# Expert stage: the choice of later experts ahead of the gate multiply on VectorE

## The chip, the cores and the metric

The kernel runs on one core of a Trainium2 chip. The metric is the time of one execution on the device, in microseconds (us). The kernel before takes 2801.93 us, the median of three runs (2798.73 to 2804.31). One execution was also profiled; rows of that profile are quoted below.

## What is computed

Two layers over 512 tokens (256 context, 256 latent). Each layer has an attention mixer and then a "PEER" expert stage. Only the second is touched here. For each token and each of 8 heads it finds the best 16 of 16,384 experts by two small searches, and sums over them:

```python
v1, i1 = lax.top_k(s1, PEER_TOPK)
v2, i2 = lax.top_k(s2, PEER_TOPK)
cand = (v1[..., :, None] + v2[..., None, :]).reshape(...)
cand_idx = (i1[..., :, None] * PEER_N_KEYS + i2[..., None, :]).reshape(...)
top_s, top_pos = lax.top_k(cand, PEER_TOPK)
expert_idx = jnp.take_along_axis(cand_idx, top_pos, axis=-1)
gates = jax.nn.softmax(top_s, axis=-1)
a = jax.nn.gelu(jnp.einsum('td,thkd->thk', tc, u_tab[ec]), approximate=False)
return jnp.einsum('thk,thkd->td', gc * a, v_tab[ec])
```

`tc` are the token's 1024 values, `ec` the chosen experts, `gc` their gates. Layer 0 does this for all 512 tokens, layer 1 for the 256 latent ones.

## The kernel before, in words

Tokens lie in chunks of 128, one token per partition. A **unit** is one head of one chunk: 16 experts per token. Layer 0 has 8 heads x 4 chunks = 32 units, layer 1 has 8 x 2 = 16, so 48 in all. Each layer's units run in a hardware loop of 4 passes (`Fori`, 8 units a pass in layer 0, 4 in layer 1). A unit's 16 experts go in 4 **groups** of 4.

The order of work is written out by hand, engine by engine, with semaphores between them:

- **POOL** (GpSimd, L833) gathers for each expert slot 128 rows of 2048 floats: 1024 of table u and 1024 of table v. The ring holds 16 slots, exactly one unit. A group's four slots are asked for again once TensorE has finished with the group (`slots_free`, L830).
- **DVE** (VectorE) does in each group four dot products of u rows with the token (L1118, each leaves a result by a short accumulator read), then waits for ScalarE's Gelu and multiplies the four values with the gates (L1124, which counts `w_ready` up), and then does one of four parts of `choose` for the unit after the next (L1125): part 0 searches the two score rows (L1019 to L1023, L1031), part 1 the 16 x 16 sums (L1033 to L1037), part 2 turns positions into indices (L1041 to L1044), part 3 forms the expert index and releases POOL (L1046 to L1049). After the fourth group it finishes the gates (L1053, L1054), copies scores where there are new ones (L1058), waits until TensorE has done the fourth group (L1131), and adds the unit's result to x (L1134, L1137).
- **ACT** (ScalarE) does the Gelu (L979) when the dots are there, waits for `w_ready`, and scales the identity by the four weights (L984): four diagonal matrices, kept for two groups.
- **PE** (TensorE) multiplies the diagonals with the v rows, 8 matmuls of 512 columns a group (L924), summing in two banks over the unit. Each such fp32 matmul stands in the profile as two instructions. Behind group 0 it also does one query projection (L886) and behind group 2 the scores (L894) in those units that have such a job (`job_of`, L763: chunk number under 2). That is 16 of the 32 units of layer 0, and all 16 of layer 1, where the projection is half as wide.

Of the kernel before, what the change touches and what calls it, by code (L numbers as in the profile page):

```python
# [42 lines left out]
def kind(c):  # L43
    return CON if c < CC else LAT
# [12 lines left out]
class Kernel:  # L57
# [637 lines left out]
    def peer(self, layer, chunks):  # L695
# [65 lines left out]
        place = [divmod(i, nch) for i in range(body + 2)]  # L761

        def job_of(i, it):  # L763

            hd, c = place[i]
            return it * 4 + (2 * hd + c + first_jobs) if c < 2 else None
# [14 lines left out]
        with nc.Block() as block:  # L781
# [221 lines left out]
            def _(dve):  # L1003
                count = [0]

                def link(ins):

                    count[0] += 1
                    ins.then_inc(chain, 1)
                    dve.wait_ge(chain, count[0])  # L1010

                def restart():

                    dve.sem_clear(chain)
                    count[0] = 0

                def top16(out_v, out_i, src):

                    link(nc.vector.max(out_v[:, 0:8], src))  # L1019
                    link(nc.vector.max_index(out_i[:, 0:8], out_v[:, 0:8], src))  # L1020
                    link(nc.vector.match_replace(src, out_v[:, 0:8], src, NEG))
                    link(nc.vector.max(out_v[:, 8:16], src))  # L1022
                    link(nc.vector.max_index(out_i[:, 8:16], out_v[:, 8:16], src))  # L1023

                def choose(par, c, u, stage):

                    if stage == 0:
                        for side in range(2):
                            top16(val[:, side, :], ind[:, side, :], scores[:, par, c, side * NKEY:(side + 1) * NKEY])  # L1030
                        link(nc.vector.tensor_copy(indf, ind))  # L1031
                    if stage == 1:
                        link(nc.vector.tensor_tensor(C, val[:, 0, :].unsqueeze(2).broadcast_to([P, TOPK, TOPK]),  # L1033
                                                     val[:, 1, :].unsqueeze(1).broadcast_to([P, TOPK, TOPK]), ALU.add))
                        top16(top, pos, C.rearrange("p a b -> p (a b)"))
                        link(nc.vector.tensor_scalar(posi[:, 0, :], pos, 4, None, ALU.logical_shift_right))
                        link(nc.vector.tensor_scalar(posi[:, 1, :], pos, TOPK - 1, None, ALU.bitwise_and))  # L1037
                    if stage == 2:
                        for side in range(2):

                            link(nc.vector.tensor_tensor(OH, posi[:, side, :].unsqueeze(2).broadcast_to([P, TOPK, TOPK]),  # L1041
                                                         iota.unsqueeze(1).broadcast_to([P, TOPK, TOPK]), ALU.is_equal))
                            link(nc.vector.tensor_tensor(OH, OH, indf[:, side, :].unsqueeze(1).broadcast_to([P, TOPK, TOPK]), ALU.mult))
                            link(nc.vector.tensor_reduce(sel[:, side, :], OH, AX.X, ALU.add))  # L1044
                    if stage == 3:
                        link(nc.vector.scalar_tensor_tensor(out=idx[:, u, :], in0=sel[:, 0, :], scalar=float(NKEY), in1=sel[:, 1, :], op0=ALU.mult, op1=ALU.add))  # L1046
                        dve.sem_inc(idx_ready, 1)
                        link(nc.vector.tensor_scalar(nb, top[:, 0:1], -1.0, None, ALU.mult))
                        dve.sem_inc(top_ready, 1)  # L1049

                def finish_gates(u):

                    link(nc.vector.reciprocal(er, es))  # L1053
                    link(nc.vector.tensor_scalar(gate[:, u, :], gate[:, u, :], er, None, ALU.mult))  # L1054

                def copy_scores(j, par, side):
                    dve.wait_ge(sc_done, j + 1)
                    nc.vector.tensor_copy(scores[:, par, 0:nch, side * NKEY:(side + 1) * NKEY],  # L1058
                                          S_BANK[:, 0:nch * NKEY].rearrange("p (c n) -> p c n", c=nch)).then_inc(sc_copied, 1)
                    dve.wait_ge(sc_copied, j + 1)  # L1060
# [48 lines left out]
                with dve.Fori(0, H // 2) as it:  # L1109
                    for i in range(body):  # L1110
                        u = i % 2
                        hd, c = place[i]
                        unit = it * body + i
                        j = job_of(i, it)
                        for g in range(NG):
                            for k in range(g * GRP, (g + 1) * GRP):
                                dve.wait_ge(gathered[k], unit * 16 + 16)
                                last = nc.vector.tensor_tensor_reduce(  # L1118
                                    out=ring[:, k, 0:D], in0=ring[:, k, 0:D], in1=self.h[:, chunks[c] * D:(chunks[c] + 1) * D], scale=1.0, scalar=0.0,
                                    op0=ALU.mult, op1=ALU.add, accum_out=a[:, u, k:k + 1])  # L1120
                            last.then_inc(dots_done, 1)
                            ks = slice(g * GRP, (g + 1) * GRP)
                            dve.wait_ge(gelu_done, unit * NG + g + 1)
                            nc.vector.tensor_tensor(w[:, u, ks], w[:, u, ks], gate[:, u, ks], ALU.mult).then_inc(w_ready, 1)  # L1124
                            choose(place[i + 2][0] % 2, place[i + 2][1], u, g)  # L1125
                        dve.wait_ge(exp_done, unit + 3)
                        finish_gates(u)
                        if j is not None:
                            copy_scores(j, (hd + lead) % 2, c)

                        dve.wait_ge(slots_free, unit * NG + 2 * NG)  # L1131
                        for n in range(2):
                            s = acc[u][n][:]
                            link(nc.vector.tensor_tensor(s, s, gate_f[:, kind(chunks[c]), n * 512:(n + 1) * 512], ALU.mult))  # L1134
                        for n in range(2):
                            xs = self.x[:, chunks[c], n * 512:(n + 1) * 512]
                            link(nc.vector.tensor_tensor(xs, xs, acc[u][n][:], ALU.add))  # L1137
                        dve.sem_inc(acc_free, 1)
                        restart()
# [270 lines left out]
```

## Time and profile before

| | |
|---|---|
| median of the runs | 2801.93 us |
| the profiled execution | 2804.31 us, its span 2804.3 us |
| expert loop of layer 0, 32 units | 1454.5 us |
| expert loop of layer 1, 16 units | 719.8 us |
| PE busy over the span | 2139.2 us (76%) |
| DVE busy over the span | 1769.5 us (63%) |
| busy share of the DMA engines in the loops | 0.92 and 0.90 |

A row of the costliest groups reads: line, engine, operation, out<-in, shape, xcount | busy us, mean ns of one | idle us of the engine just before them, and what ended most of it.
### The profile page before, as it was taken

The numbers are of one execution on the slowest core, as the hardware profiler recorded it, in microseconds if no ns is written. First come the engines' busy times: TensorE is split into PE (matmuls) and PEld (weight loads), VectorE is DVE, ScalarE is ACT, GpSimd is POOL, SyncE is SP. The second block draws the span as 40 slices with busy tenths as digits, with TensorE's granted clock in tenths as the row PEclk, the third lists the DMA queues.
The fourth block names the chain that finished last, engine by engine and source line by source line (L and its number), as shares of the span: only waits on it lengthen the run. The fifth ranks groups of instructions, "written<-read, shape, count | busy, mean of one in ns | idle before, by whom it ended". The sixth has DMA issues, their size and how long they took to land. (4 is left out here: it accounts for less than half of the span.)

```text
span 2804.3 us, 21155 instructions
## 1 busy us (share of the span) xinstructions
PE 2139.2 (76%) x5856; PEld 1008.5 (36%) x5856; DVE 1769.5 (63%) x4349; ACT 581.5 (21%) x1533; POOL 887.9 (32%) x774
## 2 busy tenths in 40 slices
PE   5899978678686878686867768678857868687776
PEld 2444443233233333232323323334533424243333
DVE  1233466867676767667585777645466767768685
ACT  1222122121112212121211121222212212122122
POOL 0000024443434434344343343400034434343431
PEclk8999989898888989898988888888968989898888
DMA  7467369998989999899998998942179999999995
GB/s 314 146 236 267 126 244 366 392 380 355 416 332 385 377 380 391 355 358 395 361 386 359 363 412 355 377 176 94 39 301 401 387 373 382 387 381 391 372 390 216
DMA packets 136073, 919.71 MB, mean 328 GB/s; under 512 B 15744, under 2 KB 20864, under 8 KB 30128
## 3 DMA queue, kind: packets, MB, share of 16 engines
q0 software_dynamic: 110592, 805.36, 71.0%
q1 hardware_dynamic: 24960, 113.03, 10.7%
q8 instruction: 24, 0.39, 0.1%
q14 instruction: 65, 0.53, 0.0%
q10 hardware_dynamic: 432, 0.40, 0.0%
HBM read 917.58 MB, written 1.15 MB: 328 GB/s over the span
## 5 line engine op out<-in xcount | busy, mean ns | idle before, releaser
L924 PE MATMUL bank<-arena,aux 128*128 128x512 f32 x3072 | 1462.6, 634 | 543.3 <-ACT aux L984 543.0
L833 POOL DMA_INDIRECT arena<-in_uv,small x768 | 887.4, 1155 | 1386.3 <-PE bank L924 1079.4
L924 PEld LDWEIGHTS bank<-arena,aux 128*128 128x128 f32 x3072 | 616.2, 204 | 1353.5 <-issue 735.8
L1118 DVE CUSTOM_DVE_ANT_0 arena<-arena,h 128x1024 f32<-128x1024 f32 x768 | 897.8, 1223 | 57.0 <-issue 36.0
L979 ACT ACTIVATE small<-small 128x4 f32<-128x4 f32 x192 | 39.5, 206 | 1466.2 <-DVE small L1118 1466.2
L984 ACT ACTIVATE aux<-ident,small 128x128 f32<-128x128 f32 x768 | 245.2, 390 | 59.6 <-DVE small L1124 58.1
L1134 DVE TENSOR_TENSOR bank<-bank,aux 128x512 f32<-128x512 f32 x96 | 67.2, 700 | 278.0 <-PE bank L924 276.3
L886 PE MATMUL bank<-hT,aux 128*128 128x512 f32 (+1 forms) x512 | 170.3, 486 | 0.0
L822 POOL IOTA small<- 128x16 int32 x2 | 0.3, 135 | 479.2 <-POOLq L53 479.2
L886 PEld LDWEIGHTS bank<-hT,aux 128*128 128x128 f32 x512 | 97.3, 190 | 74.7 <-issue 68.9
L1053 DVE RECIPROCAL small<-small 128x1 f32<-128x1 f32 x52 | 8.5, 164 | 133.7 <-ACT small L992 120.7
L847 PE MATMUL bank<-arena,hT 128*128 128x512 f32 x192 | 85.1, 603 | 3.3 <-PEq L53 3.3
L1124 DVE TENSOR_TENSOR small<-small 128x4 f32<-128x4 f32 x192 | 31.3, 163 | 73.3 <-ACT small L979 73.3
L457 PE MATMUL bank<-arena 128*128 128x512 f32 (+1 forms) x160 | 68.3, 544 | 2.1 <-PEq L53 1.4
L1137 DVE TENSOR_TENSOR x<-x,bank 128x512 f32<-128x512 f32 x96 | 65.9, 686 | 3.3
L979 ACT ACT_TABLE_LOAD x48 | 61.6, 1283 | 1.8 <-PE bank L879 1.0
L1118 DVE DVE_READ_ACCUMULATOR2_ANT small<- 128x1 f32 x768 | 61.9, 81 | 0.0
L992 ACT ACT_TABLE_LOAD x48 | 61.6, 1283 | 0.8
L532 DVE TENSOR_REDUCE small<-bank 128x1 f32<-128x512 f32 (+1 forms) x48 | 28.9, 601 | 50.7 <-PE bank L457 50.7
L1224 PE MATMUL bank<-arena,hT 128*128 128x512 f32 x128 | 58.0, 612 | 2.9 <-ACT hT L243 2.9
L656 PE MATMUL bank<-arena 128*128 128x512 f32 x128 | 56.3, 593 | 0.8 <-DVE arena L608 0.8
L1022 DVE MAX8 small<-aux 128x8 f32<-128x128 f32 x156 | 52.9, 339 | 5.4
(143 smaller groups left out, 1430.0 us busy)
## 6 DMA issues: line engine op xcount, KB each, us to landing
h<-in_ada SPq DMA_DIRECT2D x27, 1024.0 KB, 6.0
arena<-in_ada SPq DMA_DIRECT2D x21, 1024.0 KB, 6.5
aux<-in_w_query SPq DMA_DIRECT2D x36, 512.0 KB, 13.3
arena<-in_uv,small POOLq DMA_INDIRECT x768, 14.4
arena<-mod_rows SPq DMA_DIRECT2D x17, 512.0 KB, 7.0
arena<-in_w_o SPq DMA_DIRECT2D x2, 4096.0 KB, 12.3
arena<-in_w_qkv SPq DMA_DIRECT2D x3, 2048.0 KB, 10.3
arena<-in_w_in SPq DMA_DIRECT2D x2, 1536.0 KB, 8.7
```

Of the source, the lines that this page charges most:

```text
L457: last = nc.tensor.matmul(self.bank[S_BANK[u % 2]][:, 0:keys_of(c)], q, k, start=(i == 0), stop=(i == len(terms) - 1))
L833: nc.gpsimd.indirect_dma_start(out=ring[:, k, :], out_offset=None, in_=table, in_offset=bass.IndirectOffsetOnAxis(ap=idx[:, i % 2, k:k + 1 ...
L847: last = nc.tensor.matmul(self.bank[2 * (i % 2) + n][:], self.hT[:, hd, c * P:(c + 1) * P], self.w_o[:, hd, n * 512:(n + 1) * 512], start= ...
L886: last = nc.tensor.matmul(Q_BANK[:, lo:hi], wq[:, k, :], self.hT[:, k, lo:hi], start=(k == 0), stop=(k == KD - 1))
L924: last = nc.tensor.matmul(acc[i % 2][n][:], diag[:, (g % 2) * GRP + k, :], ring[:, kk, D + n * 512:D + (n + 1) * 512], start=(kk == 0), st ...
L979: nc.scalar.activation(w[:, u, ks], a[:, u, ks], ACT.Gelu).then_inc(gelu_done, 1)
L984: last = nc.scalar.mul(diag[:, (g % 2) * GRP + k, :], self.ident[:], w[:, u, g * GRP + k:g * GRP + k + 1])
L992: nc.scalar.activation(gate[:, u, :], top, ACT.Exp, bias=nb, accum_out=es).then_inc(exp_done, 1)
L1118: last = nc.vector.tensor_tensor_reduce(out=ring[:, k, 0:D], in0=ring[:, k, 0:D], in1=self.h[:, chunks[c] * D:(chunks[c] + 1) * D], scale= ...
L1134: link(nc.vector.tensor_tensor(s, s, gate_f[:, kind(chunks[c]), n * 512:(n + 1) * 512], ALU.mult))
L1137: link(nc.vector.tensor_tensor(xs, xs, acc[u][n][:], ALU.add))
L1224: last = nc.tensor.matmul(self.bank[3 * (i % 2) + n][:], self.hT[:, k, c * P:(c + 1) * P], self.w_qkv[:, n, k, :], start=(k == 0), stop=(k ...
```

## The change

In every group of a unit DVE does its part of `choose` first, and waits for the Gelu and multiplies afterwards. The two statements change places; nothing is added or taken away.

```diff
--- before.py
+++ after.py
@@ -1120,9 +1120,9 @@
                                     op0=ALU.mult, op1=ALU.add, accum_out=a[:, u, k:k + 1])
                             last.then_inc(dots_done, 1)
                             ks = slice(g * GRP, (g + 1) * GRP)
+                            choose(place[i + 2][0] % 2, place[i + 2][1], u, g)
                             dve.wait_ge(gelu_done, unit * NG + g + 1)
                             nc.vector.tensor_tensor(w[:, u, ks], w[:, u, ks], gate[:, u, ks], ALU.mult).then_inc(w_ready, 1)
-                            choose(place[i + 2][0] % 2, place[i + 2][1], u, g)
                         dve.wait_ge(exp_done, unit + 3)
                         finish_gates(u)
                         if j is not None:
```

Only DVE's order differs. In group 0 of a unit, before (the first row reads the last accumulator, ISA and REGISTER_ALU rows at L1123 or L1124 are the wait's register work, L1019 is the first row of part 0 of the choice):

```order
 L1118 ISA small 128x1
-L1123 ISA
-L1124 TENSOR_TENSOR small<-small 128x4
-L1019 MAX small<-aux 128x8
-L1020 MAX_INDEX small<-small,aux 128x8
```

and in the changed kernel, the end of the same part of the choice:

```order
+L1022 MAX small<-aux 128x8
+L1023 MAX_INDEX small<-small,aux 128x8
+L1031 CAST small<-small 128x32
+L1124 ISA
+L1125 TENSOR_TENSOR small<-small 128x4
```

The multiply (now L1125) moved behind all eleven instructions of part 0. In group 3, in the waits' own view of DVE (the names in brackets are semaphores; `chain_105` orders DVE behind itself), the multiply moved behind the two instructions of part 3:

```order
-L1123 REGISTER_ALU
-L1124 TENSOR_TENSOR small<-small 128x4 [waits gelu_done_101]
 L1046 SCALAR_TENSOR_TENSOR small<-small 128x16
 L1048 TENSOR_SCALAR small<-small 128x1 [waits chain_105]
-L1126 REGISTER_ALU [waits chain_105]
+L1124 REGISTER_ALU [waits chain_105]
+L1125 TENSOR_TENSOR small<-small 128x4 [waits gelu_done_101]
+L1126 REGISTER_ALU
 L1053 RECIPROCAL small<-small 128x1 [waits exp_done_107]
```

Behind the multiply follow, as before, the wait for the exponentials and the gates (L1053, L1054). The instructions of the other engines and their order stay as they were.

## Rows read from the trace of the kernel before

**Rows 1.** The page's part of the costliest groups; columns in the section on the profile.

```profile
L924 PE MATMUL bank<-arena,aux 128*128 128x512 f32 x3072 | 1462.6, 634 | 543.3 <-ACT aux L984 543.0
...
L1118 DVE CUSTOM_DVE_ANT_0 arena<-arena,h 128x1024 f32<-128x1024 f32 x768 | 897.8, 1223 | 57.0 <-issue 36.0
...
L1134 DVE TENSOR_TENSOR bank<-bank,aux 128x512 f32<-128x512 f32 x96 | 67.2, 700 | 278.0 <-PE bank L924 276.3
...
L1124 DVE TENSOR_TENSOR small<-small 128x4 f32<-128x4 f32 x192 | 31.3, 163 | 73.3 <-ACT small L979 73.3
```

**Rows 2.** Windows of both expert loops; busy (xcount) by engine, clock, DMA share, GB/s.

```profile
400.90:1855.40 1454.50, 1093.02 (x2432) 473.21 (x2432) 1030.00 (x2512) 291.57 (x784) 575.67 (x496) 0.88 0.92 370
2074.60:2794.40 719.80, 545.68 (x1344) 264.18 (x1344) 514.50 (x1264) 148.26 (x403) 278.81 (x240) 0.88 0.90 366
```

**Rows 3.** Timeline of PE, layer 0; start, us, engine line op [idle before].

```profile
999.37 9.75 PE L924 MATMUL bank<-arena,aux 128*128 128x512 f32 x16 [9.88 <-ACT aux L984]
1008.95 7.03 PE L886 MATMUL bank<-hT,aux 128*128 128x512 f32 x16
1015.82 13.90 PE L924 MATMUL bank<-arena,aux 128*128 128x512 f32 x32
...
1030.44 7.03 PE L924 MATMUL bank<-arena,aux 128*128 128x512 f32 x16
1047.36 16.51 PE L924 MATMUL bank<-arena,aux 128*128 128x512 f32 x32 [9.88 <-ACT aux L984]
1064.67 7.13 PE L924 MATMUL bank<-arena,aux 128*128 128x512 f32 x16 [0.80 <-ACT aux L984]
...
1089.43 16.05 PE L924 MATMUL bank<-arena,aux 128*128 128x512 f32 x32 [9.87 <-ACT aux L984]
```

**Rows 4.** Timeline of DVE over one unit, layer 0.

```profile
1040.75 1.28 DVE L1118 CUSTOM_DVE_ANT_0 arena<-arena,h 128x1024 f32<-128x1024 f32 x1 [0.36 <-DVE x L1137]
...
1045.75 0.16 DVE L1124 TENSOR_TENSOR small<-small 128x4 f32<-128x4 f32 x1 [0.27 <-ACT small L979]
1045.83 0.29 DVE L1019 MAX8 small<-aux 128x8 f32<-128x128 f32 x1
...
1049.72 1.23 DVE L1118 CUSTOM_DVE_ANT_0 arena<-arena,h 128x1024 f32<-128x1024 f32 x1
...
1054.74 0.42 DVE L1033 TENSOR_TENSOR aux<-small 128x256 f32<-128x256 f32 x1
...
1058.13 1.23 DVE L1118 CUSTOM_DVE_ANT_0 arena<-arena,h 128x1024 f32<-128x1024 f32 x1
...
1063.15 0.42 DVE L1041 TENSOR_TENSOR aux<-small 128x256 f32<-128x256 uint32 x1
...
1065.88 1.22 DVE L1118 CUSTOM_DVE_ANT_0 arena<-arena,h 128x1024 f32<-128x1024 f32 x1
...
1070.83 0.16 DVE L1124 TENSOR_TENSOR small<-small 128x4 f32<-128x4 f32 x1 [0.27 <-ACT small L979]
...
1071.23 0.15 DVE L1048 TENSOR_SCALAR small<-small 128x1 f32<-128x1 f32 x1 [0.15 <-DVE small L1046]
...
1079.60 1.43 DVE L1134 TENSOR_TENSOR bank<-bank,aux 128x512 f32<-128x512 f32 x2 [4.80 <-PE bank L924]
```

**Rows 5.** Timeline of DVE, group 2 of the unit before it.

```profile
1016.74 0.16 DVE L1124 TENSOR_TENSOR small<-small 128x4 f32<-128x4 f32 x1 [1.90 <-ACT small L979]
```

**Rows 6.** Windows, the first matmuls after an idle PE.

```profile
1047.36:1052.50 5.14, 5.14 (x6) 2.18 (x7) 4.90 (x15) 0.00 (x0) 0.00 (x0) 0.50 1.02 425
```

**Rows 7.** Timeline of PE, layer 1, first group of two units.

```profile
2125.36 9.95 PE L924 MATMUL bank<-arena,aux 128*128 128x512 f32 x16 [9.88 <-ACT aux L984]
...
2263.84 8.98 PE L924 MATMUL bank<-arena,aux 128*128 128x512 f32 x16 [15.31 <-ACT aux L984]
```

**Rows 8.** Timeline of POOL, last gather issued for that unit.

```profile
1042.02 1.97 POOL L833 DMA_INDIRECT arena<-in_uv,small  x1 [0.30 <-issue]
```

**Rows 9.** The page's DMA issues; count, median us to landing.

```profile
arena<-in_uv,small POOLq DMA_INDIRECT x768, 14.4
```

## The prediction

> **What bounds the kernel now.** I read the costliest groups first, then windows over the two expert loops, then the timelines of TensorE (PE) and VectorE (DVE) over neighbouring units.
>
> In the costliest groups the reader is to see who waits for whom [rows 1]. PE stands idle 543.3 us ahead of its expert matmuls, nearly all until ScalarE's diagonals (L984) are there. DVE stands idle 276.3 us ahead of L1134, until PE has done a unit's last group. Its 768 dot products have only 57.0 us of idle ahead of them, 36.0 of it at the restarts of the loop. So PE and DVE wait for each other in turn, and DVE hardly ever waits for a gather, though the DMA engines are busy 0.92 and 0.90 of the two loops [rows 2].
>
> The PE timeline gives the shape of a unit [rows 3]. After 9.88 us of idle PE starts group 0 at 999.37. Then come the projection at 1008.95, groups 1 and 2 from 1015.82, and group 3 from 1030.44 to its end at 1037.5, with the short scores between: one train without a gap, 38 us long. So in a unit with a projection nothing but the start of group 0 and PE's own work sets the end. In the next unit, without a projection, groups 0 and 1 are back to back (1047.36, 16.51 us), and groups 2 and 3 come after gaps such as 0.80 us, when DVE's multiply has made them ready.
>
> In the layer 0 loop 16 of 32 units have a projection. In layer 1 all 16 do, at half the width. I call these 32 units P and the other 16 units N.
>
> **What moves.** The multiply of group 0 starts at 1045.75, 0.27 us of idle after the dots, and PE starts 1.61 us behind it, at 1047.36 [rows 3, 4]. Part 0 of the choice runs from 1045.83 to the next dot at 1049.72, so it takes 3.89 us; part 1 is 1054.74 to 1058.13, 3.39; part 2 is 1063.15 to 1065.88, 2.73; part 3 is about 0.5 (1070.9 to 1071.38) [rows 4]. In the changed kernel the Gelu is long done when a part of the choice is over. The multiply of group 0 then comes 3.89 later and saves the 0.27 of waiting: a shift of **+3.62 us**, and the start of PE's group 0 shifts by as much.
>
> For the later groups, count through DVE's chain from a unit's first dot (1040.75). Before, the multiplies are at 5.0, 13.9, 22.3 and 30.1. After, each group saves its wait of 0.27 us and each multiply stands behind its own part of the choice: about 8.6, 16.8, 24.4 and 29.6. The first three are later by 3.6, 2.9 and 2.1; the last is earlier by 0.5.
>
> **Units P, 32 of them.** Their train has no gap before. After, it starts 3.62 later, and the diagonals are ready 1.6 us behind each multiply, at 18.4, 26.0 and 31.2. PE wants group 1 only behind group 0 and the projection. Group 0 takes at least 6.87 us (half of the gapless 13.90 of groups 1 and 2, less the modelled tail), and the projection 3.5 in layer 1. Even so group 1 can't start before 10.2 + 10.4 = 20.6, so the train stays whole. In layer 0 the Gelu of group 2 stands on ScalarE behind the copy of the projection, as before, where it made DVE wait 1.90 us [rows 5]. I put the multiply of group 2 there at about 27 and of group 3 at 33, which with 1.6 is still far ahead of group 3's turn at about 41. DVE's other work at the unit's end (exponentials, gates, scores) is done while it now waits for PE, and stays so. So 32 x 3.62 = **+115.8 us**.
>
> **Units N, 16 of them.** Before: DVE starts L1134 at 1079.60, 38.85 after the first dot, with PE paced by DVE's multiplies for groups 2 and 3. After: PE starts group 0 at 10.2. The two groups of 16.51 us (16.35 without the tail) and two more at 13.90 end at 10.2 + 16.35 + 13.90 = 40.5. With the shorter first pair at 1089.43 (16.05, of which a fraction was waiting for the diagonals) it is at most 40.0, and with the least slow start seen (below) 39.7. The diagonals of groups 1 to 3 (18.4, 26.0, 31.2) come at PE's turn or ahead of it, so the train becomes gapless and PE takes over as the bound. I take 40.2, so +1.4 each: 16 x 1.4 = **+22 us**. The ends are 39.7 (+0.9, 14 us) and, with the slowest start seen, 40.6 (+1.8, 28 us).
>
> **The slow start of PE.** The first 5.14 us after an idle PE run at a granted clock of 0.50, the 1.2 GHz level [rows 6]; before them the engine had been idle 9.88 us. That lengthens group 0 from 7.03 to 9.75 or 9.95 us, or to 8.98 in the shortest such row [rows 3, 7]: 1.95 to 2.92 us a unit, paid already in each of the 48. After the change the idle ahead of group 0 is 9.88 + 3.62 = 13.5 us. The row of 8.98 has 15.31 us of idle ahead of it, at a restart of the loop, and is no longer than the others. So I change nothing for it in the sum. The bounds are all starts at the least (1.95, against the middle of the two, 2.45: 48 x -0.5 = -24 us) and all at the most (48 x +0.5 = +24 us).
>
> The Trainium skill, "TensorE: Matmul & The Clock Gate", section "HAM oscillation — how this bites in real kernels", has it that each idle gap makes the next burst start cold, so that the cost goes with the number of gaps. By that rule the sum stands as it is; by a cost that grows with the gap it would be the rival on the cold start below. The two rows of layer 1 speak for the rule.
>
> **What hides it, or doesn't.** Gathers: the last gather of this unit is issued at 1042.02 and its dot starts about 1069.3, 27 us later, against a median of 14.4 to land [rows 4, 8, 9]. PE frees the groups later by 3.6 and the next unit begins later by 3.6 too, so the distance stays in P units. In N units it shrinks by up to 3 us for group 1 (freed 3.8 later, its next dots 0.9 later). The spare of about 10 us covers it. Besides, longer units ask less of the DMA engines. I put nothing in the sum; if it were not covered, the loss would be those 3 us in 16 units, +48.
>
> **Sum.** 115.8 + 22 = +138 us. Against the profiled execution (2804.31, its span 2804.3) this is 2942; its own time lies 2.4 above the median of the runs, so against the median of 2801.93 it is **2940 us**. Changes within 0.2% (5.6 us) would be no change that a measurement of this kernel can tell.
>
> **Rivals.**
>
> *The DMA engines set the pace.* At 0.92 busy they look like the most contended resource, and the order on DVE would cost nothing as long as the ring is refilled: 2802 us. For it speaks the share in rows 2. Against it speaks the idle ahead of the dots [rows 1], 57.0 us over 768 with 36.0 at restarts. The Trainium skill, "Perfetto Trace Analysis", section "Identifying the Most-Contended Engine", says to improve the resource with the highest use, for DMA by HBM utilization; no row here shows what these DMA engines can reach at most. By it alone this rival would be the forecast.
>
> *The last multiply decides (the other side).* The multiply of group 3 comes 0.5 us earlier, because four waits for the Gelu of 0.27 leave DVE's chain and part 3 of 0.5 goes in front. If each unit ended 8.8 us behind that multiply, as N units do now, every unit would be 0.5 shorter: 48 x -0.5 = -24, 2778 us. It decides from the point at which PE has a gap ahead of group 3 in spite of the later start. For it: the gap of 0.80 in the N unit [rows 3]. Against: P units have none, and in N units the start's delay of 3.6 is larger than the gaps, 0.80 and a similar one.
>
> *The cold start grows with the gap.* If the slow stretch grows as the idle does, 13.5 / 9.88, the 2.45 us become 3.35: 48 x 0.9 = +43, 2983 us. Against it is the row of 8.98.
>
> *Gathers run late in N units:* +48, 2988 us, argued above.
>
> **Chances.** My forecast 0.85; the cold start 0.06; gathers late 0.04; DMA paces 0.02; the last multiply decides 0.02, the rest 0.01 for something unseen that slows. The range holds the forecast with its bounds (24 either way for the slow start, -8 and +6 for N units) and stops short of both +43 and +48: 2912 to 2972. Slower by over 0.2% 0.96, within 0.2% 0.02, faster 0.02.
>
> **What would show it.** In the changed kernel's profile each step has its row. The idle of PE ahead of group 0 goes from 9.88 to 13.5. PE's groups 2 and 3 in N units lose their gaps. The wait of DVE ahead of the multiply falls from 73.3 us in all to that of the 16 P units of layer 0 only, some 2.5 each, 40 us. The wait of DVE ahead of L1134 rises by 3.6 to 4 in P units and by about 2 in N, from 276.3 to some 430. The loops grow to about 1535 and 778 us. The forecast is wrong if PE shows gaps behind group 0 in P units, if the matmuls at 0.50 last longer than 5.8 us a unit, or if idle until a gather stands ahead of L1118.

## The result, and the profile after

The changed kernel takes 2938.80 us (median of 4 runs, 2936.03 to 2940.17) against 2801.45 us before (4 runs). The ratio is 1.049, with a 95% interval of 1.0476 to 1.0505: 137 us slower. The forecast was 2940 us.

Costliest groups of the changed kernel, the same columns as in [rows 1]; the multiply is now L1125. L1053 and L1058 are VectorE's other two waits at a unit's end, for the exponentials and for the scores:

```profile
L924 PE MATMUL bank<-arena,aux 128*128 128x512 f32 x3072 | 1453.7, 634 | 689.5 <-ACT aux L984 689.5
...
L1118 DVE CUSTOM_DVE_ANT_0 arena<-arena,h 128x1024 f32<-128x1024 f32 x768 | 897.0, 1223 | 53.2 <-issue 37.3
...
L1134 DVE TENSOR_TENSOR bank<-bank,aux 128x512 f32<-128x512 f32 x96 | 67.2, 699 | 315.4 <-PE bank L924 313.8
...
L1053 DVE RECIPROCAL small<-small 128x1 f32<-128x1 f32 x52 | 8.5, 164 | 163.7 <-ACT small L992 161.6
L1058 DVE COPY aux<-bank 128x512 f32<-128x512 f32 (+1 forms) x32 | 17.9, 558 | 127.7 <-PE bank L894 127.7
...
L1125 DVE TENSOR_TENSOR small<-small 128x4 f32<-128x4 f32 x192 | 31.4, 164 | 77.8 <-ACT small L979 50.8
```

TensorE's idle until the diagonals grew by 146 us (543.3 to 689.5). The dots still wait for nothing: 53.2 us of idle, 37.3 of it at the loops' restarts.

Windows of the two expert loops, as in [rows 2]:

```profile
397.70:1935.00 1537.30, 1088.13 (x2432) 479.26 (x2432) 1017.76 (x2512) 291.45 (x784) 520.54 (x496) 0.85 0.87 350
2154.50:2928.70 774.20, 541.60 (x1344) 263.03 (x1344) 509.86 (x1264) 146.73 (x403) 252.11 (x240) 0.85 0.84 341
```

Layer 0 grew by 82.8 us, layer 1 by 54.4, together 137.2: all of the loss is here. Engines do the same work in more time, and the DMA engines are less busy (0.87 and 0.84).

Timeline of TensorE over the same three units as in [rows 3], one with a projection and two without:

```profile
1034.46 9.66 PE L924 MATMUL bank<-arena,aux 128*128 128x512 f32 x16 [13.51 <-ACT aux L984]
1043.96 7.03 PE L886 MATMUL bank<-hT,aux 128*128 128x512 f32 x16
1050.83 13.90 PE L924 MATMUL bank<-arena,aux 128*128 128x512 f32 x32
1064.56 1.05 PE L894 MATMUL bank<-aux 128*128 128x128 f32 x8
1065.45 7.03 PE L924 MATMUL bank<-arena,aux 128*128 128x512 f32 x16
1086.00 30.10 PE L924 MATMUL bank<-arena,aux 128*128 128x512 f32 x64 [13.51 <-ACT aux L984]
1129.61 30.48 PE L924 MATMUL bank<-arena,aux 128*128 128x512 f32 x64 [13.52 <-ACT aux L984]
```

The idle ahead of group 0 went from 9.88 to 13.51 us. In a unit without a projection the 64 matmul instructions of the four groups are now one train, 30.1 to 30.5 us; the gaps ahead of groups 2 and 3 are gone.

### The profile page after: what moved, and what is told of

Read it like the earlier page. It is cut to its first block and busy times, and to the rows that moved or that the text cites. A ratio compares the mean times of both kernels' runs of the same rounds, so it can differ in the third digit from the quotient of the medians.

```text
span 2938.4 us, 21011 instructions
## 1 busy us (share of the span) xinstructions
PE 2127.4 (72%) x5856; PEld 1013.0 (34%) x5856; DVE 1753.0 (60%) x4349; ACT 579.9 (20%) x1533; POOL 806.0 (27%) x774
## 5 line engine op out<-in xcount | busy, mean ns | idle before, releaser
L924 PE MATMUL bank<-arena,aux 128*128 128x512 f32 x3072 | 1453.7, 634 | 689.5 <-ACT aux L984 689.5
L833 POOL DMA_INDIRECT arena<-in_uv,small x768 | 805.5, 1049 | 1597.8 <-PE bank L924 1295.6
L1118 DVE CUSTOM_DVE_ANT_0 arena<-arena,h 128x1024 f32<-128x1024 f32 x768 | 897.0, 1223 | 53.2 <-issue 37.3
L1134 DVE TENSOR_TENSOR bank<-bank,aux 128x512 f32<-128x512 f32 x96 | 67.2, 699 | 315.4 <-PE bank L924 313.8
L1053 DVE RECIPROCAL small<-small 128x1 f32<-128x1 f32 x52 | 8.5, 164 | 163.7 <-ACT small L992 161.6
L1058 DVE COPY aux<-bank 128x512 f32<-128x512 f32 (+1 forms) x32 | 17.9, 558 | 127.7 <-PE bank L894 127.7
L1125 DVE TENSOR_TENSOR small<-small 128x4 f32<-128x4 f32 x192 | 31.4, 164 | 77.8 <-ACT small L979 50.8
```

The lines of the kernel that those rows point to most:

```text
L833: nc.gpsimd.indirect_dma_start(out=ring[:, k, :], out_offset=None, in_=table, in_offset=bass.IndirectOffsetOnAxis(ap=idx[:, i % 2, k:k + 1 ...
L924: last = nc.tensor.matmul(acc[i % 2][n][:], diag[:, (g % 2) * GRP + k, :], ring[:, kk, D + n * 512:D + (n + 1) * 512], start=(kk == 0), st ...
L1118: last = nc.vector.tensor_tensor_reduce(out=ring[:, k, 0:D], in0=ring[:, k, 0:D], in1=self.h[:, chunks[c] * D:(chunks[c] + 1) * D], scale= ...
```

## The experiments

The theory: VectorE's time costs only where TensorE's train waits for it. That is at group 0 in every unit, and at groups 1 to 3 only where TensorE has a gap. Rivals: each swapped group, or each unit, pays its own share; the gathers pace the kernel. Each time is the median of four or five executions; ratios and differences are to the kernel before on the same chip. The diffs are shorthand: `C(g)` is the choice's part of group g, `M(g)` the wait for the Gelu with the multiply, and names are shortened. In the variants some line numbers shift. "Read from the trace" means the time from one unit's first matmul to the next unit's, against the same unit of the kernel before, averaged over a kind of unit.

**Group 0 alone.**

```diff
-M(g); C(g)
+if g == 0: C(g); M(g)
+else:      M(g); C(g)
```

> Only in group 0 of each unit the choice goes ahead of the multiply; groups 1 to 3 are as before. Theory (the start of TensorE's train is what costs): a unit's train starts 3.62 us later and is gapless behind that, so this one swap costs as much as all four: about +137 us, 2938 us, ratio to before 1.049. Rival (each swapped group adds its share by holding the diagonals back): group 0 has 3.9 of the 10.5 us of choice in a unit, so about 0.37 of the loss, +51 us, 2852 us, ratio 1.018.

Measured: 2941.55 us, ratio 1.0495 (1.0477 to 1.0514), +138 us. One group of four costs as much as all four. Its timeline has the same train with the same idle ahead of it:

```profile
1090.80 30.10 PE L924 MATMUL bank<-arena,aux 128*128 128x512 f32 x64 [13.51 <-ACT aux L984]
```

The rival with shares is out.

**Groups 1 to 3 alone.**

```diff
-M(g); C(g)
+if g > 0: C(g); M(g)
+else:     M(g); C(g)
```

> The choice goes ahead of the multiply in groups 1 to 3 only; group 0 is as before. Theory: units with a projection lose nothing, since TensorE's turn for groups 1 to 3 comes later than their diagonals even so (18.7, 26.2 and 31.6 us after the first dot against turns at 19.7, 26.6 and 33.9 in layer 1). In the 16 units without one group 1 starts at 18.7 in place of 15.5 and the train ends at 39.9 in place of 38.85: 16 x 1.05 = +17 us, 2818 us, ratio 1.006. Rival (every group its share): 0.63 of the loss, +86 us, 2888 us, ratio 1.031.

Measured: 2841.96 us, ratio 1.0134 (1.0114 to 1.0153), +39 us, and 1.0132 when it was run again. It is nearer to the theory than to the rival, but twice the +17 us. Read from the trace, the units with a projection lost about 0.1 us each and those without one 2.1 us, not 1.05. TensorE in one of the latter, by timeline and by windows (granted clock is the third figure from the end):

```profile
1059.25 9.57 PE L924 MATMUL bank<-arena,aux 128*128 128x512 f32 x16 [9.87 <-ACT aux L984]
1071.29 22.41 PE L924 MATMUL bank<-arena,aux 128*128 128x512 f32 x48 [2.47 <-ACT aux L984]
```

```profile
1071.30:1073.00 1.70, 1.70 (x2) 0.82 (x3) 1.70 (x3) 0.00 (x0) 1.40 (x2) 0.50 0.80 236
...
1075.00:1078.50 3.50, 3.50 (x9) 1.52 (x8) 3.24 (x9) 1.05 (x4) 0.58 (x1) 1.00 0.97 379
```

The later diagonals opened a gap of 2.47 us between groups 0 and 1, and group 1 began at the 1.2 GHz level, a second slow start in one unit. I had not reckoned with it. The trace has it in 14 of the 16 units, after gaps of 2.36 to 2.52 us. In the other two the gap was longer, 2.81 and 2.96 us, and group 1 took 7.13 us, at a granted clock of 1.00:

```profile
512.18 7.13 PE L924 MATMUL bank<-arena,aux 128*128 128x512 f32 x16 [2.81 <-ACT aux L984]
```

The two partial swaps do not add up to the whole (138 and 39 us against 137). Once group 0 starts late, the later groups' diagonals are there in time.

**The gap filled.** To test that, TensorE does three useless matmuls in that gap, in the kernel with groups 1 to 3 swapped.

```diff
+if j is None and g == 0:
+    for k in range(3):
+        matmul(Q_BANK[:, lo:hi], hT[:, k, 0:P], hT[:, k, lo:hi], start=(k == 0), stop=(k == 2))
```

> As the kernel with groups 1 to 3 swapped (2842 us), and in the 16 units without a projection TensorE does three more matmuls of 512 columns (six instructions, some 2.6 us, result used by nobody) in the gap of 2.47 us between groups 0 and 1. Theory (the gap let the granted clock fall to 0.50 again, which made group 1 take 8.4 us in place of 6.9, on top of its later start): without the gap group 1 runs at full clock, each of these units ends about 1.0 us earlier, 2842 - 16 = 2826 us, ratio to before about 1.008. Rival (group 1 is slow for another reason, such as gathers landing beside it or the diagonals): 2842 us or a little more, ratio 1.0135.

> The kernel with groups 1 to 3 swapped once more, on the same chip as the filled gap, to compare the two: 2842 us, ratio 1.0135.

Measured: 2823.87 us, ratio 1.0082 (1.0069 to 1.0096), against 2838.12 us and 1.0132 (1.0116 to 1.0147) without them. More work on TensorE made the kernel 14 us faster. Its timeline (L931 are the added matmuls):

```profile
1057.89 2.74 PE L931 MATMUL bank<-hT 128*128 128x512 f32 x6
1060.80 7.13 PE L924 MATMUL bank<-arena,aux 128*128 128x512 f32 x16 [0.17 <-ACT aux L987]
```

Group 1 takes 7.13 us now, at a granted clock of 1.00. Read from the trace, the units without a projection lost 2.0 us each without the added matmuls (2.1 in the first run) and 1.3 with them. So the second slow start was most of the missing 1 us a unit; what the remaining 0.2 us are stays open.

**Only the units without a projection**, all four groups swapped.

```diff
-M(g); C(g)
+if j is None: C(g); M(g)     # j is None: no projection in this unit
+else:         M(g); C(g)
```

> All four groups swapped, but only in the 16 units of layer 0 that have no projection. Theory: TensorE has gaps of 0.6 to 0.8 us ahead of groups 2 and 3 there, which take up most of the 3.62 us; what is left is about 1.5 us a unit, 16 x 1.5 = +24 us, 2825 us, ratio 1.0086. Rival (each unit loses its full shift): 16 x 3.62 = +58 us, 2859 us, ratio 1.021.

Measured: 2829.70 us, ratio 1.0095 (1.0078 to 1.0112), +26 us. This is the prediction's term of 22 us by itself, 4 us above it; the rival's 58 is out.

**Extra work behind the multiply.**

```diff
 M(g)
+if g == 0:
+    for _ in range(8): link(tensor_tensor(OH, C, C, ALU.max))
 C(g)
```

> The order of before, with eight more VectorE operations of 256 columns (0.46 us each, 3.66 together, their result is used by nobody) behind the multiply of group 0. Theory (VectorE's time costs only where TensorE's train waits for it): units with a projection in layer 0 lose nothing; in layer 1 the diagonals of group 3 come at 35.4 against a turn at 33.9, +1.4 each, 16 x 1.4 = 22; the 16 units without projection lose all of it, 16 x 3.66 = 59. Together +81 us, 2882 us, ratio 1.029. Rival (VectorE's time adds up in every unit, wherever it stands): 48 x 3.66 = +176 us, 2977 us, ratio 1.063.

Measured: 2895.67 us, ratio 1.033 (1.0314 to 1.0346), +92 us. By kind of unit, read from the trace as before: layer 0 with a projection +0.1 us each, layer 1 +1.9, without a projection +3.8. The same 3.66 us of VectorE cost nearly nothing in 16 units and all of themselves in 16 others. The 11 us beyond the forecast are 8 in layer 1, where I had set the diagonals against the slowest turn seen (33.9), not the mean one, and, in all, some 2 us in each of the two other kinds.

**Extra work ahead of the multiply**, in the changed kernel.

```diff
 C(g)
+if g == 0:
+    for _ in range(8): link(tensor_tensor(OH, C, C, ALU.max))
 M(g)
```

> The changed kernel with the same eight extra VectorE operations (3.66 us, result unused) ahead of the multiply of group 0, behind part 0 of the choice. Theory: now all 48 trains are gapless, so each unit ends later by the full 3.66: 48 x 3.66 = +176 us on the changed kernel, 3115 us, ratio to before 1.112. The slow start of TensorE stays at 1.9 to 2.9 us a unit although the idle ahead of it grows to 17 us. Rival (the slow start grows with the idle, in proportion): another 48 x 0.9 = +43 us, 3158 us, ratio 1.127. Rival (units without projection still have room): 32 x 3.66 = +117 us, 3056 us.

Measured: 3116.87 us, ratio 1.1116 (1.1099 to 1.1133), +313 us. With the change's own 137 us taken off, that leaves 313 - 137 = 176 us, on average 3.66 for each of the 48 units. Read from the trace it is 3.4 in layer 0 and 3.9 in layer 1: the idle ahead of group 0 grew by 3.67 (13.51 to 17.18), and the slow starts differ a little. TensorE over one unit without a projection:

```profile
1140.77 29.84 PE L924 MATMUL bank<-arena,aux 128*128 128x512 f32 x64 [17.18 <-ACT aux L984]
```

After 17.18 us of idle the train takes no longer than after 13.51. Over all units with a projection, group 0 took on average 9.49 us before, 9.45 in the changed kernel and 9.18 here in layer 0, and 9.60, 9.35 and 9.56 in layer 1. A cold start that grows with the gap is out.

**Taking the sum out later.** VectorE takes a unit's sum out of the banks behind group 0 of the next unit, once with the order of before and once with the changed one. The first call finds banks set to zero.

```diff
-dve.sem_inc(acc_free, 2)
+memset(acc[1][n], 0.0) for both n; dve.sem_inc(acc_free, 1)
 ...
+if g == 0:
+    take_out((i - 1) % body, unit * NG + NG)
 ...
-dve.wait_ge(slots_free, unit * NG + 2 * NG)
-(L1132 to L1138: the gate, the sum, acc_free)
+take_out(body - 1, H * nch * NG + NG)   # behind the loop
```

> The order of before, but VectorE takes a unit's sum out of the banks (L1134, L1137) behind group 0 of the next unit, not ahead of it. Theory (the hand-off at the unit's end, TensorE's 9.9 us of idle, is what a later start adds to): with it gone, VectorE's own chain is some 38 us a unit (34.1 to the gates, 3.3 for the sum, 1 for the scores) and the gathers some 42 (16.8 MB, and 17.3 with a projection, at the 391 GB/s of the busiest units), so the gathers take over as the bound: about 48 x 42.3 + 35 at the loops' restarts = 2065 us for the two loops in place of 2174, 2690 us in all, ratio 0.96. If gathers reach 425 GB/s it is VectorE, near 39.5 us a unit, and 2565 us. Rival (the gathers bound the kernel already, at a DMA share of 0.92): within 1% of before.

> The same later take-out, in the changed kernel's order. Theory: the 3.62 us on the start of a train are hidden, since TensorE is no longer what a unit ends with; within 1% of the kernel that takes out later with the order of before (about 2690 us), ratio to before about 0.96. Rival (the start of each train is paid for whatever comes ahead of it): 32 x 3.62 + 22 = +138 us above that kernel, 2828 us, ratio 1.01.

Measured: 2629.77 us, ratio 0.9377 (0.9364 to 0.939), with the order of before, and 2633.46 us, ratio 0.9392 (0.9379 to 0.9405), with the changed one. Both are 6% faster than the kernel before. The order that cost 137 us costs 4 here. The two intervals overlap, though all five times of the one (2627.83 to 2631.88) lie below all five of the other (2632.51 to 2636.44), so the 4 us may be real. The windows from 600 to 1600 us of the kernel before, and of this one with the order of before:

```profile
600.00:1600.00 1000.00, 747.98 (x1674) 324.76 (x1673) 698.13 (x1705) 200.06 (x535) 404.91 (x350) 0.88 0.93 373
```

```profile
600.00:1600.00 1000.00, 840.44 (x1827) 361.56 (x1826) 777.65 (x1889) 220.55 (x588) 410.15 (x384) 0.92 1.01 415
```

The costliest groups of the latter (L1133 are the dots):

```profile
L1133 DVE CUSTOM_DVE_ANT_0 arena<-arena,h 128x1024 f32<-128x1024 f32 x768 | 907.3, 1223 | 178.3 <-DMA arena<-in_uv,small 118.8
```

Now the dots wait for gathers, 118.8 us. The Trainium skill, "DMA: Bandwidth & Descriptors", section "Where 436 GB/s comes from", has it that transfers between HBM and SBUF are bound near 358 GB/s a core, which it works out as half of what the memory gives to two cores. This kernel runs on one core, and the 415 GB/s of this window are above that figure; the measurement decides.

## Why the prediction was right

**The start of group 0.** +3.62 us were worked out; the idle ahead of it grew by 3.63. The first multiply of a unit comes 8.6 us after the first dot, as forecast, and the swap in group 0 alone gives the whole loss. (For group 2 the prediction has 24.4; its own terms give 24.2, and so does the trace.)

**Units with a projection.** Forecast 32 x 3.62 = 115.8 us. Read from the trace, in layer 0 each grew by 3.6, in layer 1 the loop grew by 54.4 us, 3.4 a unit. So 58 + 54 = 112. The trains kept whole. The missing 4 us are slow starts: a group 0 in layer 1 took about 0.25 us less on average than before, 9.35 us, which is 2.32 above the 7.03 at full clock and within the bounds given (1.95 to 2.92). Single ones are not: the shortest took 8.57 us. Already the trace before has one of 8.76, so the 8.98 that the prediction took for the shortest was not.

**Units without one.** Forecast +1.4 each; the layer 0 loop's growth of 82.8 less 58 leaves 25, +1.55 each, and by itself the term measured +26. The trains are gapless, as forecast.

**The sum.** 112 + 25 = 137 against 138. The two terms erred by 4 and 3 us in opposite senses; that the sum came this close is luck, while each term by itself held. The range had a slip at its low end: with both lower bounds (24 and 8 us) it would begin at 2908, not 2912. It did not matter here.

**The gathers.** They stayed off the path (53.2 us of idle ahead of the dots), and the later take-out shows where they come on it. There my own estimate was off: I took 391 GB/s for what the busiest units could get and forecast 2690 us; the gathers reached 415, and it was 2630.

**Waits that I split wrongly.** Forecast for L1134 was an idle of some 430 us; it is 315.4. VectorE's longer wait for TensorE is shared out over three places in a row at the unit's end: L1053 (120.7 us before by the list of waits, 161.6 after), L1058 (40.8 and 127.7) and L1134 (276.3 and 313.8). Their sum grew from 437.8 to 603.1. The time of the whole did not hang on it, but a reader who looked at L1134 alone would have seen a quarter of the growth. The wait for the Gelu, forecast at 40 us, is 50.8: in the 16 units it is 3.40 us in the one that I looked at, not 2.5.

**The rival on the other side** had the last multiply 0.5 us earlier, which it is (29.6 in place of 30.1 after the first dot), but no unit has a gap ahead of group 3 in which that would count.

## What to carry to other kernels

Find the first hand-off of each repeated unit: if the engine that takes it then works without a gap, every microsecond put ahead of that hand-off is paid in full, and what stands behind it is free as long as the taker finds its next work ready. Filling the producer's short wait (here 0.27 us) with 3.9 us of other work is a loss wherever a consumer waits on what follows. And before ordering work around such a hand-off, ask whether the hand-off itself can be overlapped with the previous unit: that gave 6% here and left 4 of the 137 us that the order had cost.

## What the runs showed of the hardware

- A gap of 2.47 us on TensorE, one group after a slow start, was followed by a granted clock of 0.50; filling such gaps gave back 0.8 us a unit. Gaps of 0.80 to 1.38 us did not lengthen the group behind them (7.13 us). The length of the gap alone does not decide it: gaps of 2.81 and 2.96 us in the same kernel, and of 3.23 to 3.58 us in four units of the kernel with the extra work behind, were followed by 7.13 us as well. What decides stays open here. A gap of 3.23 us in layer 0 of that kernel, and one of 1.27 us in its layer 1:

```profile
511.05 7.13 PE L924 MATMUL bank<-arena,aux 128*128 128x512 f32 x16 [3.23 <-ACT aux L984]
...
2209.03 7.13 PE L924 MATMUL bank<-arena,aux 128*128 128x512 f32 x16 [1.27 <-ACT aux L984]
```

- The slow start is no longer after 13.5 or 17.2 us of idle than after 9.9: in the units with a projection group 0 took 9.55 us on average in the kernel before, 9.40 in the changed kernel and 9.36 in the one with the extra work ahead.
- A DMA share of 0.93 in a window was not the limit: the same gathers reached 1.01 and 415 GB/s once asked for sooner.
